# Decay gates of a gated linear attention: products in column and row groups, another copy on VectorE, and a new order of the first products

## The chip, the cores and the metric

The kernel runs on one core of a Trainium2 chip. The metric is the time of one execution on the device in microseconds (us). Three runs of the kernel before took 1970.91, 1971.70 and 1971.77; their median is 1971.7.

## The reference, cut to what matters

Two transformer blocks over 256 latent tokens of width 1024, all in float32. The first block reads 256 context tokens besides. Its mixer starts from one wide projection of the modulated, normalised tokens:

```python
h  = modulate(rms_norm(x_lat, norm1_g), sh1, sc1)      # latent tokens
hc = modulate(rms_norm(x_ctx, norm1_g), sh1c, sc1c)    # context tokens
q_c, kv_c, k_rope, gq, gk, gv, gr, glow, gate_logits = split_columns(h @ w_in)
# latent attention (MLA): q from rms_norm(q_c) @ w_uq, k and v from rms_norm(kv_c) @ w_ukv
lf, lb = glow[..., :16], glow[..., 16:]                # low-rank input of the decays, two directions
g_f = log_sigmoid(lf @ w_decay[0] + b_decay[0]) / 16   # 512 columns each
g_b = log_sigmoid(lb @ w_decay[1] + b_decay[1]) / 16
```

The decays g_f and g_b are summed over chunks and drive the gated linear attention (GLA). A feed-forward with a convolution follows. The second block has an attention, an mLSTM, a pooling mixer and two mixtures of 16 experts whose weights (2 x 16 x 12 MB) are all read.

## The kernel before, in words

Each engine runs one program written out by hand in its order; semaphores join them. Work waits for what stands ahead of it on its engine, so the order of the code is the order of time.

- **Banks.** `Groups` hands PSUM banks to products in turn: four in the first ring, four in a second one (`second=True`). `open` waits until the bank's last reader has given it back, `close` counts a product as done, `take` makes a reader wait for the product, `give` frees the bank, `read` waits until a bank has been given back.
- **Weights.** SyncE sends them in a fixed list into a ring of six slots of 2 MB. Each load waits until the product that last used its slot is done (`G.over`), or, where VectorE sums modulation columns itself (`mod_sum`), for that sum. The queue is in order.
- **First products.** TensorE transposes the tokens, forms four modulation rows (`mod`, L501) as their weights come, and sums squares (`norm`, L526). VectorE multiplies hT by gain and inverse root in tiles of 128 channels (L1787), latent tokens first; ScalarE adds the shift (L1389). Then come `kvr` (288 columns, four blocks of 128 tokens; blocks 0 and 1 are latent, 2 and 3 context), its root on ScalarE (L1423) and scaling on VectorE (L1837), transposes (`kvt`), `w_ukv` (eight products of two steps), `qc` (384 columns, latent blocks only), transposes of k and q, `w_uq`, rotary embedding. Ordinary chains of products all have line 475, transposes line 483.
- **Attention** over eight heads: scores (L555), softmax on VectorE and ScalarE, transposes (L483), outputs (L565), with products gk and gv as filling.
- **GLA.** After gv and gq, `low` is one product of 32 columns with all 512 tokens moving. VectorE copies it to SBUF (L1932) beside a row of ones, and the decays z (L696) are eight products of 33 rows: 16 of one direction, 16 of the other (zero weights stand where the other direction's are), and the bias. Each of the eight fills one bank; all eight banks are in use. For each half of four, ScalarE forms |z| (L1493), exp(-|z|) (L1495) and ln(1 + .) (L1496), and VectorE min(z,0) minus that, reading z from its bank (L1945) and giving it back. The product `gr` (L475, 64 instructions of 256 columns) takes the first four banks again. Then `tot` (L711) and the chunk sums.

A float32 product shows in the trace as two matmul instructions, so x64 are 32 products.

Of the kernel before, what the change touches and what calls it, by code (L numbers as in the profile page):

```python
# [8 lines left out]
ACT = mybir.ActivationFunctionType  # L9
ALU = mybir.AluOpType  # L10
# [3 lines left out]
D = 1024  # L14
KD = D // 128
# [238 lines left out]
def build(nc, w, consts, out):  # L254
# [3 lines left out]
    with ctx:  # L258
# [66 lines left out]
        sq_late = ar(0, KD, T)  # L325
        mrow = ar(17536, 512)

        kvr = ar(0, 4, 288)
# [17 lines left out]
        gex = ar(10240, 2, 512)  # L346
        wdec = ar(11264, 1024)
        qeT = ar(11264, 2, 4 * T)
        keT = ar(13312, 2, 4 * T)
        low = ar(15360, 512)  # L350
        dtm = ar(15872, 512)
        st = [ar(15360, 2, 512), ar(10240, 2, 512)]
        atT = ar(0, 8, 128)
        atM = ar(1024, 2, 256)
# [110 lines left out]
        def w3(v, k, n):  # L465
            return v[:, 0:k * n].rearrange("p (k n) -> p k n", k=k)
# [4 lines left out]
        def _(pe):  # L471
# [69 lines left out]
            def normed(c, k=KD):  # L541
                pe.wait_ge(sem("normed"), KD * (c - (c > 4)) + k)
# [60 lines left out]
            x = w3(weights(pe, "kvr"), KD, 288)  # L603
            for tb in range(4):
                if tb % 2 == 0:
                    normed(tb // 2)
                token_major("kvr", x, 288, tb)
            G.over("kvr")
            for j in range(2):
                b = G.open(pe, ("kvt", j))  # L610
                pe.wait_ge(sem("kv_norm"), 4)
                turn(("kvt", j), b, [kvr[:, tb, j * 128:j * 128 + 128] for tb in range(4)])
# [8 lines left out]
            G.over("w_ukv")  # L621
            x = w3(weights(pe, "qc"), KD, Q_LORA)
            for tb in range(TB):
                token_major("qc", x, Q_LORA, tb)
            G.over("qc")
            pe.wait_ge(sem("k_rope"), 4)
# [59 lines left out]
            b = G.open(pe, "low")  # L686
            chain("low", b[0:32, :], lambda k: x[:, k, :], lambda k: hT[:, k, :], KD)
            G.over("low")
            mod_columns(11)

            pe.wait_ge(sem("decay_in"), 3 * 16)
            pe.wait_ge(sem("low_ready"), 1)
            for tb in range(4):
                for d in range(2):
                    b = G.open(pe, ("z", tb, d), second=tb >= 2)
                    G.close(pe.matmul(b, low[0:33, tb * 128:tb * 128 + 128], wdec[0:33, d * 512:d * 512 + 512],  # L696
                                      start=True, stop=True), ("z", tb, d))
            x = w3(weights(pe, "gr"), KD, 512)
# [8 lines left out]
            for tb in range(TB):  # L707
                for d in range(2):
                    G.read(pe, ("z", tb, d))
                    r = 32 * (2 * tb + d)  # L710
                    ins = pe.matmul(b[r:r + 32, :], c_("chunk_pick"), gg[:, tb, d * 512:d * 512 + 512],  # L711
                                    start=True, stop=True, skip_group_check=True)
            G.close(ins, "tot")

            def context_sums(tb, d):
                b = G.open(pe, ("aft", tb, d))
                far = (tb, d) in ((2, 0), (3, 1))
                G.read(pe, ("z", tb, d))
                ins = pe.matmul(b, c_(("sum_after", "sum_before")[d]), gg[:, tb, d * 512:d * 512 + 512],
                                start=True, stop=not far)  # L720
                if far:
                    G.read(pe, ("z", 5 - tb, d))
                    ins = pe.matmul(b, c_("sum_all"), gg[:, 5 - tb, d * 512:d * 512 + 512], start=False, stop=True)
                G.close(ins, ("aft", tb, d))
# [627 lines left out]
        def _(act):  # L1352
# [23 lines left out]
            def root(c, then=None):  # L1376

                b = G.take(act, ("ms", c))
                if c:
                    act.wait_ge(sem("scaled"), KD * c)  # L1380
                G.give(act.activation(rs, b[:, 0:T], ACT.Sqrt, bias=eps, scale=1.0 / D), ("ms", c))
                if then:
                    act.activation(small[:, 4:5], one, then)
# [29 lines left out]
            squares(1, xcT)  # L1413
            for i in (1, 2, 3):
                mod(i)
            shift(0, mc(0, 0), hT[:, :, 0:T])
            root(1)
            shift(1, mc(0, 0, 1), hT[:, :, T:2 * T])
# [8 lines left out]
            for tb in range(4):  # L1427
                rms_root("kvr", tb, KV_LORA, KV_LORA, 8)
            for j in range(2):
                evict(("kvt", j), kvT[:, j, :], ACT.Copy, scale=vc("kv_norm_g", j))  # L1430
            for tb in range(4):
# [3 lines left out]
                G.give(act.copy(v_tm[:, tb, 256:512].rearrange("p (h c) -> p h c", h=4), v[:, :, NOPE:]), ("kv", tb, 1))  # L1435
            for tb in range(TB):
                rms_root("qc", tb, Q_LORA, Q_LORA, 12)
            for h in (1, 3):
# [41 lines left out]

            act.wait_ge(sem("wdec_cleared"), 1)
            act.dma_start(wdec[0:16, 0:512], w["gla_w_decay"][0, 0]).then_inc(sem("decay_in"), 16)
            act.dma_start(wdec[16:32, 512:1024], w["gla_w_decay"][0, 1]).then_inc(sem("decay_in"), 16)
            act.dma_start(wdec[32:33, :], w["gla_b_decay"].rearrange("a b c -> a (b c)")).then_inc(sem("decay_in"), 16)
            evict(("gv", 3), gv[:, 3, :])
            mod(12)
            evict(("gq", 1), gq[:, 1, :], scale=128 ** -0.5)
            mod(13)

            for half in range(2):  # L1490
                for tb in (2 * half, 2 * half + 1):
                    for d in range(2):
                        link(act.activation(gg[:, tb, d * 512:d * 512 + 512], G.take(act, ("z", tb, d)), ACT.Abs))  # L1493
                g = gg[:, 2 * half:2 * half + 2, :]
                link(act.activation(g, g, ACT.Exp, scale=-1.0))  # L1495
                act.activation(g, g, ACT.Ln, bias=one).then_inc(sem("gate_log"), 1)  # L1496
# [226 lines left out]
        def _(dve):  # L1723
# [54 lines left out]

            def invert(c):
                G.read(dve, ("ms", c))  # L1780
                link(dve.reciprocal(rs, rs))

            def norm(c, src, g, dst):
                if c:
                    invert(c)
                for k in range(KD):
                    dve.scalar_tensor_tensor(dst[:, k, :], src[:, k, :], g[:, k:k + 1], rs,  # L1787
                                             ALU.mult, ALU.mult).then_inc(sem("scaled"), 1)
# [33 lines left out]
            invert(0)  # L1822
            for i in (1, 2, 3):
                mod(i)
            set_gain(0, mc(0, 1), vc("norm1_g", 0, KD))
# [15 lines left out]
            for tb in range(4):  # L1841
# [6 lines left out]
                if tb < TB:  # L1848
                    link(rope(src.rearrange("p (n x h q) -> p n x h q", n=1, x=2, h=2),
                              src.rearrange("p (n x h q) -> p n x h q", n=1, x=2, h=2), "rope32", tb, small[:, 128:384], 1, 8))  # L1850
                dve.tensor_copy(kcat[:, tb, :].rearrange("p (h c) -> p h c", h=MLA_H)[:, :, NOPE:],
                                src.unsqueeze(1).to_broadcast([128, MLA_H, ROPE])).then_inc(sem("k_rope"), 1)
            for tb in range(4):
                b = G.take(dve, ("kv", tb, 0))
                v = b.rearrange("p (h c) -> p h c", h=4)
                dve.tensor_copy(kcat[:, tb, 0:4 * QH].rearrange("p (h c) -> p h c", h=4)[:, :, 0:NOPE], v[:, :, 0:NOPE])
                G.give(dve.tensor_copy(v_tm[:, tb, 0:256].rearrange("p (h c) -> p h c", h=4), v[:, :, NOPE:]), ("kv", tb, 0))
            for tb in range(TB):
                low_rank("qc", tb, qc[:, tb, :], Q_LORA, 12, "q_norm")
                dve.sem_inc(freed[G.bank[("qc", tb)]], 1)  # L1860
            for h in (0, 2):
# [58 lines left out]

            dve.memset(wdec[0:33, :], 0.0).then_inc(sem("wdec_cleared"), 1)
            mod_sum(10, 0, KD)
# [7 lines left out]
            b = G.take(dve, "low")  # L1930
            dve.memset(low[32:33, :], 1.0)
            G.give(dve.tensor_copy(low[0:32, :], b[0:32, :]), "low")  # L1932
            G.read(dve, "low")
            dve.sem_inc(sem("low_ready"), 1)
            mod_columns(11)
            for i in range(4, 12):
                G.read(dve, ("mod_t", i))

            def log_gates(half):

                dve.wait_ge(sem("gate_log"), half + 1)
                for tb in (2 * half, 2 * half + 1):
                    for d in range(2):
                        g = gg[:, tb, d * 512:d * 512 + 512]
                        G.give(dve.scalar_tensor_tensor(g, G.take(dve, ("z", tb, d)), 0.0, g, ALU.min, ALU.subtract),  # L1945
                               ("z", tb, d))

            log_gates(0)
            for j in range(3):
# [538 lines left out]
```

## Time and profile before

| | |
|---|---|
| runs, us | 1970.91, 1971.70, 1971.77 |
| profiled execution, us | 1969.03 |
| its span, us | 1967.2 |
| busy, us: TensorE, VectorE, ScalarE | 1654.7, 627.3, 406.9 |
| TensorE's mean granted clock | 0.903 |

The span runs from the first to the last instruction of the profiled execution; its own time is 1.8 us more. Busy time says how long an engine worked, not whether the end waited for it. The clock is given as a share of 2.4 GHz.

### The profile page before, as it was taken

Reading aid. Unit: us, or ns where it says so; the run is one execution under the profiler, and the core shown is the slowest. Engines: PE = TensorE matmul, PEld = TensorE weight load, DVE = VectorE, ACT = ScalarE, POOL = GpSimd, SP = SyncE. Lnnn points to the kernel's source line nnn. Section 1 sums busy time; section 2 is a strip of 40 time slices with the busy share of each in tenths; the row PEclk is TensorE's granted clock in tenths of the full one; section 3 lists DMA queues with packets and bytes.
Section 4 is the critical chain, followed back from the end, with each engine's and each line's share of the span. In section 5 each row is a group of like instructions: output and inputs, shape, how many; then the busy total and the mean of one; then the engine's idle time right before and its main releaser. Section 6 shows DMA issues by size and latency. Waiting matters only on the chain.

```text
span 1967.2 us, 22134 instructions
## 1 busy us (share of the span) xinstructions
PE 1654.7 (84%) x9130; PEld 1060.5 (54%) x9130; DVE 627.3 (32%) x1467; ACT 406.9 (21%) x717; POOL 18.6 (1%) x26
## 2 busy tenths in 40 slices
PE   6999999989999999996889676677687976776776
PEld 4544457878888886553645243243245533433433
DVE  3267344127798436546221000000024100000001
ACT  3221151011220023212132121121123211211211
POOL 0000000000110000000000000000000000000000
PEclk8999899999999999887879898898897988888888
DMA  9525740265639825105589999999996999999996
GB/s 366 179 98 202 282 162 1 86 221 186 218 125 359 320 101 206 43 1 215 224 336 430 428 429 428 429 429 428 428 366 256 397 429 428 429 428 429 428 428 262
DMA packets 110759, 572.47 MB, mean 291 GB/s; under 512 B 9153, under 2 KB 15425, under 8 KB 86114
## 3 DMA queue, kind: packets, MB, share of 16 engines
q1 hardware_dynamic: 109776, 569.79, 71.9%
q10 hardware_dynamic: 914, 1.72, 0.3%
q8 instruction: 49, 0.80, 0.2%
q14 instruction: 20, 0.16, 0.0%
HBM read 570.44 MB, written 1.05 MB: 291 GB/s over the span
## 4 chain that ended last, share of the span: by engine, by line
PE 61%; DMA 30%; DVE 4%; ACT 2%; issue 1%; SPq 1%; DVEq 0%; ACTq 0%
DMA ring<-in_w_exp_up_dram 29%; PE bank L475 20%; PE bank L1155 9%; PE bank L858 8%; PE bank L885 4%; PE bank L483 2%; PE bank L1181 2%; PE bank L1231 1%; PE bank L1191 1%; PE bank L901 1%; PE bank L555 1%; PE bank L501 1%; PE bank L526 1%; PE bank L1142 1%; DMA ring<-in_w_ada_dram 1%
## 5 line engine op out<-in xcount | busy, mean ns | idle before, releaser
L1155 PE MATMUL bank<-ring,arena 128*32 128x512 f32 x1792 | 264.1, 744 | 194.2 <-DMA ring<-in_w_exp_up_dram 192.2
L1155 PEld LDWEIGHTS bank<-ring,arena 128*32 128x32 f32 x1792 | 69.6, 133 | 386.1 <-issue 349.9
L2422 DVE COPY arena<-bank 128x256 f32<-128x256 f32 x32 | 13.6, 425 | 601.6 <-PE bank L1171 601.6
L475 PE MATMUL bank<-ring,hT 128*128 128x512 f32 (+4 forms) x480 | 163.6, 498 | 6.5 <-issue 4.9
L858 PE MATMUL bank<-hT,ring 128*128 128x256 f32 x704 | 156.5, 385 | 4.2 <-ACT hT L1389 4.2
L858 PEld LDWEIGHTS bank<-hT,ring 128*128 128x128 f32 x704 | 135.4, 193 | 23.3 <-issue 4.6
L475 PEld LDWEIGHTS bank<-ring,hT 128*128 128x128 f32 x480 | 88.1, 195 | 77.4 <-issue 67.3
L1181 PE MATMUL bank<-ring,arena 128*32 128x512 f32 x960 | 124.6, 664 | 1.7 <-DVE arena L2426 1.7
L1689 ACT COPY arena<-bank 128x512 f32<-128x512 f32 x32 | 33.4, 1045 | 435.9 <-PE bank L1155 435.9
L1191 PE MATMUL bank<-arena 128*128 128x256 f32 x512 | 118.8, 385 | 1.8 <-DVE arena L2434 1.8
L1761 DVE SCALAR_TENSOR_TENSOR spare<-ring,spare 128x512 f32<-128x512 f32 x154 | 116.3, 755 | 4.4
L1191 PEld LDWEIGHTS bank<-arena 128*128 128x128 f32 x512 | 94.6, 190 | 39.8 <-issue 28.2
L1142 PE MATMUL bank<-arena 128*128 128x32 f32 x960 | 110.2, 274 | 0.0
L1142 PEld LDWEIGHTS bank<-arena 128*128 128x128 f32 x960 | 110.1, 193 | 0.0
L475 PE MATMUL bank<-hT,ring 128*128 128x256 f32 (+1 forms) x464 | 109.8, 396 | 0.2 <-DVE arena L1945 0.2
L475 PE MATMUL bank<-arena,ring 128*128 128x256 f32 x416 | 97.2, 389 | 5.2 <-DVE arena L2012 3.5
L475 PEld LDWEIGHTS bank<-hT,ring 128*128 128x128 f32 (+1 forms) x464 | 88.8, 192 | 23.1 <-issue 10.9
L483 PE MATMUL bank<-cst,arena 128*128 128x128 f32 (+2 forms) x382 | 63.8, 311 | 41.9 <-DVE arena L1899 11.6
L2046 DVE SCALAR_TENSOR_TENSOR arena<-arena,vcol 128x256 f32<-128x256 f32 x176 | 91.9, 522 | 6.3
L475 PEld LDWEIGHTS bank<-arena,ring 128*128 128x128 f32 x416 | 81.2, 196 | 17.9 <-issue 4.8
L483 PEld LDWEIGHTS bank<-cst,arena 128*128 128x128 f32 (+2 forms) x382 | 49.8, 156 | 75.2 <-issue 64.2
L1365 ACT ACTIVATE arena<-bank 128x256 f32<-128x256 f32 (+2 forms) x72 | 32.3, 453 | 244.4 <-PE bank L475 136.4
(332 smaller groups left out, 1673.5 us busy)
## 6 DMA issues: line engine op xcount, KB each, us to landing
ring<-in_w_exp_down_dram SPq DMA_DIRECT2D x60, 2048.0 KB, 18.9
ring<-in_w_exp_gate_dram SPq DMA_DIRECT2D x56, 2048.0 KB, 19.0
ring<-in_w_exp_up_dram SPq DMA_DIRECT2D x56, 2048.0 KB, 23.4
ring<-in_w_mod_dram SPq DMA_DIRECT2D x24, 2048.0 KB, 12.4
ring<-in_w_ada_dram SPq DMA_DIRECT2D x12, 2048.0 KB, 13.2
ring<-in_w_up_dram SPq DMA_DIRECT2D x10, 2048.0 KB, 11.1
ring<-in_w_in_dram SPq DMA_DIRECT2D x8, 2048.0 KB, 13.6
arena<-in_w_exp_up_dram SPq DMA_DIRECT2D x6, 2048.0 KB, 22.6
```

Of the source, the lines that this page charges most:

```text
L475: ins = pe.matmul(b, lhs(k), rhs(k), start=(k == 0), stop=(k == n - 1))
L483: ins = pe.transpose(b[0:m, j * p:j * p + p], src, ident[0:p, 0:p])
L858: ins = pe.matmul(b[:, 0:T], x[:, k, j * 128:j * 128 + 128], hT[:, k, 0:T], start=(k == 0), stop=(k == KD - 1))
L885: ins = pe.matmul(acc[n // 2][:, (n % 2) * T:(n % 2) * T + T], x[:, k, n * 128:n * 128 + 128], ff[:, j, :], start=(j == 0 and n % 2 == 0), ...
L1142: ins = pe.matmul(bank[0][:, k * CAP:(k + 1) * CAP], h_tm[:, tb, k * 128:k * 128 + 128], hot[:, tb, :], start=(k + tb == 0), stop=(k == KD ...
L1155: ins = pe.matmul(bank[0][32 * q:32 * q + 32, :], xe[:, k * CAP:(k + 1) * CAP], xs[q // 2][:, o:o + 512], start=(k == 0), stop=(k == KD - ...
L1181: ins = pe.matmul(bank[2 + h][32 * q:32 * q + 32, :], act_t[:, 4 * j + q, :], x[:, q, h * 512:h * 512 + 512], start=(j == 0), stop=(j == 1 ...
L1191: ins = pe.matmul(acc[n // 2][:, (n % 2) * T:(n % 2) * T + T], dsb[:, n // 4, (n % 4) * 128:(n % 4) * 128 + 128], gates, start=False, stop ...
L1365: G.give(act.activation(to, src, func, **kw), name)
L1689: act.copy(gu.rearrange("p (k c) -> p c k", k=4), bank[0].rearrange("p (c k) -> p c k", k=4)).then_inc(sem("gu_copied"), 1)
L1761: ins = dve.scalar_tensor_tensor(a, x[:, k, :], cond[:, which, k, 0:1], a, ALU.mult, ALU.add)
L2046: ins = dve.scalar_tensor_tensor(y, win, tap(i, j), y, ALU.mult, ALU.add)
```

## The change

1. `kvr` is done tile by tile: both latent blocks of a channel tile as soon as that tile is ready, then both context blocks.
2. `qc` moves ahead of `kvt` and `w_ukv`, on TensorE, ScalarE and VectorE alike.
3. The root of the context norm gets a tile of its own (`rs_ctx`) and moves ahead of modulations 2 and 3, as does its reciprocal.
4. `low` is formed in four column groups: group 2 * par + d holds direction d for the token blocks of parity par. Four copies (two on VectorE, two on ScalarE) take it to SBUF, where a memset has put ones.
5. The decay weights and biases are loaded four times, once under each group, in eight loads instead of three. The products z have 17 rows at partitions 0, 32, 64, 96 in turn.
6. VectorE copies min(z,0) of each decay product to SBUF behind its |z| (`clip_gates`, for both halves ahead of `log_gates`) and gives the bank back there. `log_gates` then subtracts SBUF from SBUF. ScalarE no longer waits between one |z| and the next.

```diff
@@ TensorE, first products
-            for tb in range(4):
-                if tb % 2 == 0:
-                    normed(tb // 2)
-                token_major("kvr", x, 288, tb)
+            for half in range(2):
+                bs = [G.open(pe, ("kvr", 2 * half + t)) for t in range(2)]
+                for k in range(KD):
+                    normed(half, k + 1)
+                    for t in range(2):
+                        tb = 2 * half + t
+                        ins = pe.matmul(bs[t][:, 0:288], hT[:, k, tb * 128:tb * 128 + 128], x[:, k, 0:288],
+                                        start=(k == 0), stop=(k == KD - 1))
+                        if k == KD - 1:
+                            G.close(ins, ("kvr", tb))
             G.over("kvr")
+            x = w3(weights(pe, "qc"), KD, Q_LORA)
+            for tb in range(TB):
+                token_major("qc", x, Q_LORA, tb)
+            G.over("qc")
@@ TensorE, low and z
-            chain("low", b[0:32, :], lambda k: x[:, k, :], lambda k: hT[:, k, :], KD)
+            for k in range(KD):
+                for r in range(4):
+                    par, d = r // 2, r % 2
+                    tokens = hT[:, k, :].rearrange("p (a b t) -> p a b t", a=2, b=2)[:, :, par, :]
+                    ins = pe.matmul(b[32 * r:32 * r + 16, 0:T], x[:, k, 16 * d:16 * d + 16], tokens,
+                                    start=(k == 0), stop=(k == KD - 1), skip_group_check=True)
+            G.close(ins, "low")
...
-            pe.wait_ge(sem("decay_in"), 3 * 16)
+            pe.wait_ge(sem("decay_in"), 8 * 16)
             pe.wait_ge(sem("low_ready"), 1)
+            pe.wait_ge(sem("low_ready_too"), 2)
             for tb in range(4):
                 for d in range(2):
+                    r, at_ = 32 * (2 * (tb % 2) + d), tb // 2 * 128
                     b = G.open(pe, ("z", tb, d), second=tb >= 2)
-                    G.close(pe.matmul(b, low[0:33, tb * 128:tb * 128 + 128], wdec[0:33, d * 512:d * 512 + 512],
-                                      start=True, stop=True), ("z", tb, d))
+                    G.close(pe.matmul(b, low[r:r + 17, at_:at_ + 128], wdec[r:r + 17, :], start=True, stop=True), ("z", tb, d))
@@ ScalarE
             root(0)
             squares(1, xcT)
-            for i in (1, 2, 3):
-                mod(i)
+            mod(1)
+            root(1)
+            mod(2)
+            mod(3)
             shift(0, mc(0, 0), hT[:, :, 0:T])
-            root(1)
...
-            act.wait_ge(sem("wdec_cleared"), 1)
-            act.dma_start(wdec[0:16, 0:512], w["gla_w_decay"][0, 0]).then_inc(sem("decay_in"), 16)
-            act.dma_start(wdec[16:32, 512:1024], w["gla_w_decay"][0, 1]).then_inc(sem("decay_in"), 16)
-            act.dma_start(wdec[32:33, :], w["gla_b_decay"].rearrange("a b c -> a (b c)")).then_inc(sem("decay_in"), 16)
+            for r in range(4):
+                d = r % 2
+                act.dma_start(wdec[32 * r:32 * r + 16, :], w["gla_w_decay"][0, d]).then_inc(sem("decay_in"), 16)
+                act.dma_start(wdec[32 * r + 16:32 * r + 17, :], w["gla_b_decay"][0, d:d + 1]).then_inc(sem("decay_in"), 16)
...
+            b = G.take(act, "low")
+            act.wait_ge(sem("low_set"), 1)
+            for r in (2, 3):
+                act.copy(low[32 * r:32 * r + 16, :], b[32 * r:32 * r + 16, 0:T]).then_inc(sem("low_ready_too"), 1)
...
-                        link(act.activation(gg[:, tb, d * 512:d * 512 + 512], G.take(act, ("z", tb, d)), ACT.Abs))
+                        act.activation(gg[:, tb, d * 512:d * 512 + 512], G.take(act, ("z", tb, d)), ACT.Abs).then_inc(
+                            sem("gate_abs"), 1)
+                act.wait_ge(sem("gate_abs"), 4 * half + 4)
@@ VectorE
-            dve.memset(wdec[0:33, :], 0.0).then_inc(sem("wdec_cleared"), 1)
+            dve.memset(low, 1.0).then_inc(sem("low_set"), 1)
...
-            dve.memset(low[32:33, :], 1.0)
-            G.give(dve.tensor_copy(low[0:32, :], b[0:32, :]), "low")
-            G.read(dve, "low")
+            dve.wait_ge(sem("low_set"), 1)
+            dve.tensor_copy(low[0:16, :], b[0:16, 0:T])
+            link(dve.tensor_copy(low[32:48, :], b[32:48, 0:T]))
             dve.sem_inc(sem("low_ready"), 1)
+            dve.wait_ge(sem("low_ready_too"), 2)
+            dve.sem_inc(freed[G.bank["low"]], 1)
...
+            def clip_gates(half):
+
+                for n in range(4 * half, 4 * half + 4):
+                    tb, d = n // 2, n % 2
+                    dve.wait_ge(sem("gate_abs"), n + 1)
+                    G.give(dve.tensor_scalar(z_low[n], G.take(dve, ("z", tb, d)), 0.0, None, ALU.min), ("z", tb, d))
+
             def log_gates(half):
...
-                        G.give(dve.scalar_tensor_tensor(g, G.take(dve, ("z", tb, d)), 0.0, g, ALU.min, ALU.subtract),
-                               ("z", tb, d))
...
+                    dve.tensor_tensor(g, z_low[n], g, ALU.subtract).then_inc(sem("log_gates"), 1)
+            clip_gates(0)
+            clip_gates(1)
             log_gates(0)
```

## Rows read from the trace of the kernel before

**Rows 1.** The page, part 4: the chain that ended last, shares by engine

```profile
PE 61%; DMA 30%; DVE 4%; ACT 2%; issue 1%; SPq 1%; DVEq 0%; ACTq 0%
```

**Rows 2.** The chain of waits in order of time: start us, us, what

```profile
44.09 18.84 PE bank L475 x64
...
64.74 0.64 PE bank L483 x4
...
66.81 26.00 PE bank L475 x64
92.84 0.59 ACT small L1423 x2
...
97.49 7.99 PE bank L475 x24
...
117.48 6.87 PE bank L475 x16
...
1063.48 34.72 DMA ring<-in_w_exp_up_dram
```

**Rows 3.** Waits of the SyncE queue, 0 to 320 us: total us, times, longest

```profile
SPq L1273 <- PE bank L475: 134.4, 9, 29.1
```

**Rows 4.** Timeline, 0 to 112 us: start us, us, engine, line, operation [idle before]

```profile
17.70 3.76 SPq L1273 DMA_DIRECT2D ring<-in_w_in_dram  x1
...
33.95 3.23 PE L501 MATMUL bank<-ring,spare 128*32 128x512 f32 x16 [2.86 <-DMA ring<-in_w_ada_dram]
...
40.17 3.25 DVE L1787 SCALAR_TENSOR_TENSOR hT<-xT,gain,rs 128x256 f32<-128x256 f32 x8
40.69 3.30 ACT L1389 ACTIVATE hT<-hT,modc 128x256 f32<-128x256 f32 x8 [2.23 <-DVE hT L1787]
...
82.32 10.48 PE L475 MATMUL bank<-ring,hT 128*128 128x384 f32 x32
```

**Rows 5.** DMA issues of kvr's weights: KB, median us from issue to landing

```profile
ring<-in_w_in_dram SPq DMA_DIRECT2D x1, 1152.0 KB, 19.2
```

**Rows 6.** Stretches: us, busy by engine (instructions), granted clock, DMA share, GB/s

```profile
50.00:51.00 1.00, 1.00 (x5) 0.83 (x4) 0.00 (x0) 0.00 (x0) 0.00 (x0) 0.86 1.05 387
...
62.93:66.81 3.88, 1.06 (x8) 0.88 (x9) 1.13 (x4) 2.04 (x5) 0.00 (x0) 1.00 0.69 208
107.20:108.30 1.10, 0.04 (x2) 0.06 (x2) 1.10 (x4) 0.58 (x1) 0.00 (x0) 1.00 0.91 315
...
227.57:234.55 6.98, 6.98 (x17) 1.67 (x16) 0.16 (x1) 0.00 (x0) 0.00 (x0) 1.00 1.05 387
...
238.00:251.60 13.60, 13.40 (x21) 6.03 (x20) 2.48 (x4) 11.09 (x12) 0.00 (x0) 0.50 0.92 348
```

**Rows 7.** The chain of waits again, 225 to 305 us

```profile
227.64 6.98 PE bank L475 x16
...
248.44 15.65 PE bank L475 x64
...
270.44 0.99 PE bank L711 x8
...
301.61 1.09 PE bank L792 x16
```

**Rows 8.** Timeline, 234 to 262 us

```profile
235.29 0.68 DVE L1932 COPY arena<-bank 32x512 f32<-32x512 f32 x1
...
236.12 12.12 PE L696 MATMUL bank<-arena 33*128 33x512 f32 x16 [0.52 <-issue]
...
237.25 0.60 ACT L1493 ACTIVATE arena<-bank 128x512 f32<-128x512 f32 x1 [9.71 <-PE bank L696]
...
247.28 2.46 ACT L1493 ACTIVATE arena<-bank 128x512 f32<-128x512 f32 x4
247.60 2.48 DVE L1945 SCALAR_TENSOR_TENSOR arena<-bank,arena 128x512 f32<-128x512 f32 x4 [11.33 <-ACT arena L1496]
...
254.27 2.00 ACT L1496 ACTIVATE arena<-arena,small 128x2048 f32<-128x2048 f32 x1
```

More of the change, by code:

```diff
@@ L326, in build @@
         mrow = ar(17536, 512)
+        rs_ctx = ar(16512, T)
         kvr = ar(0, 4, 288)
@@ L346, in build @@
         gex = ar(10240, 2, 512)
-        wdec = ar(11264, 1024)
+        wdec = ar(11264, 512)
         qeT = ar(11264, 2, 4 * T)
         keT = ar(13312, 2, 4 * T)
-        low = ar(15360, 512)
+        low = ar(15360, T)
         dtm = ar(15872, 512)
         st = [ar(15360, 2, 512), ar(10240, 2, 512)]
+        z_low = [ar(11776 + 512 * i, 512) for i in range(7)] + [ar(10240, 512)]
         atT = ar(0, 8, 128)
@@ L621, in _ @@
             G.over("w_ukv")
[L622 to L625, printed above, removed]
             pe.wait_ge(sem("k_rope"), 4)
@@ L708, in _ @@
                 for d in range(2):
-                    G.read(pe, ("z", tb, d))
+                    pe.wait_ge(sem("log_gates"), 2 * tb + d + 1)
                     r = 32 * (2 * tb + d)
@@ L717, in context_sums @@
                 far = (tb, d) in ((2, 0), (3, 1))
-                G.read(pe, ("z", tb, d))
+                pe.wait_ge(sem("log_gates"), 2 * tb + d + 1)
                 ins = pe.matmul(b, c_(("sum_after", "sum_before")[d]), gg[:, tb, d * 512:d * 512 + 512],
@@ L721, in context_sums @@
                 if far:
-                    G.read(pe, ("z", 5 - tb, d))
+                    pe.wait_ge(sem("log_gates"), 2 * (5 - tb) + d + 1)
                     ins = pe.matmul(b, c_("sum_all"), gg[:, 5 - tb, d * 512:d * 512 + 512], start=False, stop=True)
@@ L1378, in root @@
                 b = G.take(act, ("ms", c))
-                if c:
+                if c > 1:
                     act.wait_ge(sem("scaled"), KD * c)
-                G.give(act.activation(rs, b[:, 0:T], ACT.Sqrt, bias=eps, scale=1.0 / D), ("ms", c))
+                G.give(act.activation(rs_ctx if c == 1 else rs, b[:, 0:T], ACT.Sqrt, bias=eps, scale=1.0 / D), ("ms", c))
                 if then:
@@ L1428, in _ @@
                 rms_root("kvr", tb, KV_LORA, KV_LORA, 8)
+            for tb in range(TB):
+                rms_root("qc", tb, Q_LORA, Q_LORA, 12)
             for j in range(2):
@@ L1435, in _ @@
                 G.give(act.copy(v_tm[:, tb, 256:512].rearrange("p (h c) -> p h c", h=4), v[:, :, NOPE:]), ("kv", tb, 1))
-            for tb in range(TB):
-                rms_root("qc", tb, Q_LORA, Q_LORA, 12)
             for h in (1, 3):
@@ L1779, in invert @@
             def invert(c):
+                r = rs_ctx if c == 1 else rs
                 G.read(dve, ("ms", c))
-                link(dve.reciprocal(rs, rs))
+                link(dve.reciprocal(r, r))
             def norm(c, src, g, dst):
-                if c:
+                if c > 1:
                     invert(c)
                 for k in range(KD):
-                    dve.scalar_tensor_tensor(dst[:, k, :], src[:, k, :], g[:, k:k + 1], rs,
+                    dve.scalar_tensor_tensor(dst[:, k, :], src[:, k, :], g[:, k:k + 1], rs_ctx if c == 1 else rs,
                                              ALU.mult, ALU.mult).then_inc(sem("scaled"), 1)
@@ L1822, in _ @@
             invert(0)
-            for i in (1, 2, 3):
-                mod(i)
+            mod(1)
+            invert(1)
+            mod(2)
+            mod(3)
             set_gain(0, mc(0, 1), vc("norm1_g", 0, KD))
@@ L1852, in _ @@
                                 src.unsqueeze(1).to_broadcast([128, MLA_H, ROPE])).then_inc(sem("k_rope"), 1)
+            for tb in range(TB):
+                low_rank("qc", tb, qc[:, tb, :], Q_LORA, 12, "q_norm")
+                dve.sem_inc(freed[G.bank[("qc", tb)]], 1)
             for tb in range(4):
@@ L1857, in _ @@
                 G.give(dve.tensor_copy(v_tm[:, tb, 0:256].rearrange("p (h c) -> p h c", h=4), v[:, :, NOPE:]), ("kv", tb, 0))
-            for tb in range(TB):
-                low_rank("qc", tb, qc[:, tb, :], Q_LORA, 12, "q_norm")
-                dve.sem_inc(freed[G.bank[("qc", tb)]], 1)
             for h in (0, 2):
@@ L1937, in _ @@
                 G.read(dve, ("mod_t", i))
+            def clip_gates(half):
[3 more added lines that the diff above has]
+                    G.give(dve.tensor_scalar(z_low[n], G.take(dve, ("z", tb, d)), 0.0, None, ALU.min), ("z", tb, d))
             def log_gates(half):
                 dve.wait_ge(sem("gate_log"), half + 1)
-                for tb in (2 * half, 2 * half + 1):
-                    for d in range(2):
-                        g = gg[:, tb, d * 512:d * 512 + 512]
-                        G.give(dve.scalar_tensor_tensor(g, G.take(dve, ("z", tb, d)), 0.0, g, ALU.min, ALU.subtract),
-                               ("z", tb, d))
+                for n in range(4 * half, 4 * half + 4):
+                    tb, d = n // 2, n % 2
+                    g = gg[:, tb, d * 512:d * 512 + 512]
+                    G.read(dve, ("z", tb, d))
+                    dve.tensor_tensor(g, z_low[n], g, ALU.subtract).then_inc(sem("log_gates"), 1)
+            clip_gates(0)
+            clip_gates(1)
             log_gates(0)
```

## The prediction

> **What bounds the kernel now.** I read the shares of the chain of waits first: TensorE holds 61% of it, DMA 30% [rows 1]. Then the chain in order of time. From 1063 us on it alternates with waits for expert weights [rows 2]; ahead of that, DMA stands in it only at the start, where the last modulation weights arrive at 33.95 us [rows 4]. Between the two the SyncE queue waits for TensorE [rows 3], so loads follow the products: time saved early moves everything behind it forward, the expert stream too. All edits lie between 33.95 and 270.44 us, so the question is how much earlier the product "tot" (L711) starts.
>
> **First products (kvr, w_ukv, qc).** The first product starts at 44.09 [rows 2], when all eight latent tiles are ready. VectorE scales from 40.17, ScalarE shifts eight tiles from 40.69 in 3.30, 0.41 each [rows 4]. With a wait per tile the first one is enough: 40.69 + 0.41 = 41.10, 2.99 us earlier. The weights were issued at 17.70 and landed 19.2 later, at 36.9 [rows 4, 5]: no new wait. One tile now feeds two blocks, four instructions. 64 take 18.84, in the mean 0.29, so at least 1.2 us per tile against 0.41 from ScalarE: the pacing costs nothing. The context root and reciprocal move ahead of modulations 2 and 3, into the wait for DMA that ends at 33.95; the context tiles are ready near 47.3, and TensorE asks for them near 52.
>
> The clock was at half level (1.2 GHz) from the start of this product to 50.3 (mean 0.86 in 50 to 51), then full [rows 6]. I take the slow stretch, 6.2 us, as equally long after the earlier start: gain 2.99. If it ends at the same moment, the extra 3 us are half wasted: 1.5. If there is none, 3.1 more: 6.1.
>
> Behind it TensorE waited from 44.09 + 18.84 = 62.93 to 64.74 for the last kv normalisation, then 2.07 for transposes and two evictions until 66.81 [rows 2]. Now qc (10.48 us [rows 4]) stands there and hides the normalisation: +1.81. But ScalarE takes qc's root first (0.59 for the squares [rows 2], with the root 0.9), where the evictions used to begin 0.66 behind the first transpose: 2.3 instead of 2.07, -0.24. Behind w_ukv the last kv eviction now stands open ahead of the kT transposes; in return qc's own root and scaling are gone there. I add 0.85 to the eviction's end, 1.7 for four heads' transposes (16 at 0.43/4), 0.65 for a kT eviction, 1.35 for three of qcT: 4.55, against 97.49 - 66.81 - 26.00 = 4.68 [rows 2]. Gain 0.1.
>
> w_ukv started at half clock: 66.81 to 82.32 is 15.51 [rows 2, 4], where 32 instructions at 0.429 (16 in 6.87 [rows 2]) make 13.74. Ahead of it TensorE had worked 1.06 of 3.88 us [rows 6]. The hole is now 2.3 us, right behind 10 us of dense work; a hole of 1.1 us between transposes left the clock at 1.00 [rows 6]. I take full clock, +1.77; bounds 1.77 and -1.7 (slow twice as long). Sum so far: 2.99 + 1.81 - 0.24 + 1.77 + 0.1 = 6.4.
>
> The stretch from 62.93 to 66.81 held eight transposes, and half clock followed. The Trainium skill, "TensorE: Matmul & The Clock Gate", Part 4: PE-mode transpose, says that transposes do not count as the engine being busy in the same way. By that rule the new hole is longer than it looks, and the slow start of w_ukv may stay; that is among the rivals, worked out from the rows above.
>
> SyncE's loads: the slot of w_ukv, free at 82.3 before, comes free at its new end near 86.5, and the load behind it (qc's slot, free since 70) queues there. Attention starts near 104.5, and VectorE wants these columns several products later. Hidden, with over 20 us to spare.
>
> **Attention** is not touched. The decay loads behind it grow from three issues to eight on ScalarE's queue, some 0.5 each, 4 us. ScalarE's next work is the eviction of a product of 16 instructions (6.87 [rows 2]) that starts at the same time: hidden; without that cover 2.5.
>
> **Low product.** 16 instructions of 512 columns took 6.98 [rows 7]. Now there are 64 of 256 columns in four column groups: one by one 64 x 0.2145 = 13.7, four at a time 3.4. Column groups do run together: L711, 128x32 tiles of 512 columns, does 8 in 0.99 [rows 7], where 0.429 each would make 3.4. But no row that I read has pairs closer than L792, 16 in 1.09, 68 ns each [rows 7]. I take 64 x 0.068 = 4.35, nearest to that row: gain 2.63. Bounds 3.4 (gain 3.6) and 0.99/8 = 124 ns, 7.9 (loss 0.9).
>
> The Trainium skill, "TensorE: Matmul & The Clock Gate", Part 1, gives about 62 ns per matmul where software decodes; by that page an estimate would be 4.0 us. The row's 68 ns decides here.
>
> The copies of low: before, 234.62 (227.64 + 6.98) to 236.12, a memset and a copy of 0.68 for 512 columns in it [rows 7, 8]. Now the memset is done long before, and VectorE makes two copies of 256 columns, ScalarE two beside them; at 0.4 each 1.1 in all, bounds 0.8 and 1.5. Gain 0.4.
>
> **Decay products and gates, the largest term.** Call the start of z Z, 236.12 before. "gr" started at 248.44, Z + 12.32 [rows 7], because it needed the bank of z(0,0), which VectorE began to release at 247.60, after Abs, Exp and Ln of the half [rows 8]. Now VectorE's copy of min(z,0) releases it: first Abs at 237.25, Z + 1.13, 0.60 long; the copy 0.7, like L1945, which also reads 512 columns of a bank (2.48 for four) [rows 8]; 0.2 of semaphores: Z + 2.6. z itself must be done by then. Sixteen instructions at 0.429 are 6.9 one by one, 1.7 in four row groups, 3.4 at half clock or with only two overlapping, which would cost 0.8. L792 shows two row groups overlapping: 68 ns for a 128-column instruction, for which 0.429/4 = 107 is the time by itself [rows 7]. I take 2.6: gain 9.7. Bounds: 0.2 (z takes 12.1 as before [rows 8]) and 9.7.
>
> Behind that, gr to tot took 270.44 - 248.44 = 22.0 [rows 7], kept. Half clock held from 238.0 to 251.6 [rows 6], so gr began with 3.2 us of it. I keep its 15.65. Bounds 13.8 (full clock) and 17.1 (slow as long as the first product was).
>
> What is late next: the gates. The second half, with four Abs in a row and two table loads, took from 247.28 to 256.27, 9.0 [rows 8]; the first can't take longer now. So its Ln ends by Z + 1.1 + 9.0 = Z + 10.1, the second by Z + 19.1. VectorE's copies of the second half wait for its Abs (until Z + 13.3), with log_gates(0) (2.5) and three gr evictions queued behind them: done by Z + 17.2. log_gates(1) ends by Z + 21.7, gr 3 and modulation 13 behind it. tot is due at Z + 2.6 + 22.0 = Z + 24.6: 3 us of slack. The eight extra copies on VectorE (8 x 0.62 = 5) hide under it; without it the second half's would cost 2.5. gr's four banks hold their products until VectorE comes; modulation 14 wants the first near Z + 18.3, free by Z + 16.3.
>
> Total: 6.4 + 2.6 + 0.4 + 9.7 = 19.1. The profiled execution took 1969.03 (span 1967.2): 1949.9. The median of the runs, 1971.7, lies 2.7 above it; by the median 1952.6.
>
> **Rivals.**
> Small losses together: the clock's dip at w_ukv stays (1.8), the low product gains nothing (2.6) and gr is slow for 6.2 us (1.4): 1958.4. For it: the rows show it at both levels, and I can't time its changes. The dip alone makes 1954.4; I give it 0.35 by itself.
> Row groups do not overlap: a tile of 17 rows is a form that no row has. z takes 12 us at half clock again, gr gains 0.2: 1952.6 + 9.5 = 1962.1. Against it: L792.
> Slower: tiles of 16 columns and of 17 rows run one after another, at half clock. The low product takes 64 x 0.429 = 27.5, 20.5 more than before; z as just said. -6.4 - 0.4 - 0.2 + 20.5 = +13.5: 1985.2. Where z does not overlap either, it decides from (6.98 + 7.0)/64, about 220 ns per pair, on. Against it: L711 at 124 ns for 512 columns, and the clock stayed at 1.00 through 6.98 us of 32-column tiles [rows 6, 7].
> No effect: something I missed between 60 and 270 binds, say VectorE's sums at the end of attention. Against it: the products of the chain stand back to back there. Within 3.9 of before.
>
> **How the numbers follow.** Forecast 0.6 (own range 1948 to 1956), small losses 0.25, row groups 0.08, no effect 0.03, slower 0.04. Low end: gr at full clock (1.9), the low product in 3.4 (0.9) and an earlier rise of the clock in the first product (1.7) give 1948.1. High end between the second and third case, 1961. About 0.2% (3.9 us) is what a measurement tells from no change: faster 0.93, same 0.03, slower 0.04.
>
> **What would show it.** The first product from 41.1 with qc right behind it; w_ukv 2.3 behind qc, in 13.7; low, 64 instructions in 4.3; gr within 3 us of z; tot about 19 earlier; the first wait for expert weights at about 1044 instead of 1063. It would be wrong if gr starts at the old distance, if low lasts over 7 us, or if tot waits for VectorE.

## The result, and the profile after

The changed kernel takes 1951.05 us (median of four runs, 1948.14 to 1954.61) against 1971.31 for the kernel before (four runs, 1966.35 to 1971.77). The ratio is 0.9903, 95% interval 0.9886 to 0.9919: 19 us faster, between 16 and 22. The forecast was 1952.6. The profiled execution took 1950.72, its span is 1948.7, 18.5 less than before.

Part 4 of the page of the profile has the same shares as before, 61% for TensorE and 30% for DMA. Here is the chain of waits in order of time (start us, us, what). L477, L485, L503, L528, L557 and L567 are the helper lines that were L475, L483, L501, L526, L555 and L565; L612 is kvr, L699 the low product, L517 columns of a modulation, L712 the decay products z, L1439 ScalarE's squares of qc, L726 tot.

```profile
11.63 20.62 DMA ring<-in_w_ada_dram
...
39.79 18.55 PE bank L612 x64
58.34 10.33 PE bank L477 x32
68.69 0.59 ACT small L1439 x2
...
70.90 13.99 PE bank L477 x32
...
89.59 7.99 PE bank L477 x24
...
219.56 3.58 PE bank L699 x64
223.14 0.98 PE bank L517 x8
...
224.26 2.28 PE bank L712 x16
226.57 0.70 DVE arena L1971
...
227.41 16.89 PE bank L477 x64
...
250.65 1.00 PE bank L726 x8
...
305.78 79.13 PE bank L477 x352
...
1044.98 34.67 DMA ring<-in_w_exp_up_dram
```

The stage is shorter in the same kind of chain [rows 1]. qc (x32, 10.33) stands directly behind kvr, w_ukv (13.99) 2.23 behind qc, and gr 3.15 behind z, where it had stood 12.32 behind [rows 2, 7]. The same points of both chains, in us:

| from, to | before | after | gain | forecast |
|---|---|---|---|---|
| 0, arrival of the last modulation weights | 33.91 | 32.25 | 1.66 | 0 |
| first product starts | 10.18 | 7.54 | 2.64 | 2.99 |
| w_uq starts | 53.40 | 49.80 | 3.60 | 3.44 |
| low starts | 130.15 | 129.97 | 0.18 | 0 |
| z starts | 8.48 | 4.70 | 3.78 | 3.03 |
| gr starts | 12.32 | 3.15 | 9.17 | 9.7 |
| tot starts | 22.00 | 23.24 | -1.24 | 0 |
| end of the span | 1696.76 | 1698.05 | -1.29 | 0 |
| sum | 1967.2 | 1948.7 | 18.5 | 19.1 |

The 1.66 is the DMA's own variation: nothing of the change lies ahead of it, and in the fourteen profiles of this study that arrival lies between 32.2 and 34.3, in no order that follows the kernels. The last loss is in one piece, x352, with 77.91 before and 79.13 here. The mean clock over that stretch was 0.98 before and 0.96 after; these are the lines (us, busy by engine, granted clock, DMA share, GB/s), first before, then after:

```profile
325.58:404.59 79.01, 77.89 (x352) 67.95 (x352) 10.20 (x24) 5.38 (x14) 0.00 (x0) 0.98 0.14 54
```

```profile
305.78:386.02 80.24, 79.12 (x353) 68.79 (x353) 10.20 (x24) 5.38 (x14) 0.00 (x0) 0.96 0.14 53
```

The clock falls earlier there: 1.2 us into the piece before, but already in the wait ahead of it in the changed kernel, so that 5.9 us of the piece are at half clock instead of 3.3.

```profile
324.00:326.00 2.00, 0.42 (x2) 0.43 (x3) 1.29 (x2) 0.00 (x0) 0.00 (x0) 1.00 0.00 0
```

```profile
304.00:306.00 2.00, 0.22 (x1) 0.25 (x2) 1.46 (x3) 0.00 (x0) 0.00 (x0) 0.71 0.00 0
```

This loss goes with the one at gr. In the seven profiles of this study where gr takes 16.6 to 17.0 us, x352 takes 78.98 to 79.20; in the other seven, where gr takes 14.05 to 15.9, it takes 77.91. Kernels with the old gates and with the new ones stand on both sides, so it follows the clock and not the form of the gates. Why the one follows the other 60 us later no run shows.

From there on both chains run in step: the first wait for expert weights comes 18.50 earlier [rows 2], the end 18.5. Where the time went at gr, the stretches show:

```profile
224.00:226.50 2.50, 2.36 (x18) 1.35 (x17) 0.21 (x2) 1.11 (x3) 0.00 (x0) 0.97 1.03 380
226.50:228.00 1.50, 0.62 (x3) 0.54 (x3) 1.43 (x3) 1.47 (x3) 0.00 (x0) 0.50 1.05 388
...
232.00:234.00 2.00, 2.00 (x9) 1.63 (x8) 0.78 (x2) 2.00 (x4) 0.00 (x0) 0.71 1.05 387
```

The clock falls to 1.2 GHz at 226.4, at the end of z, and rises near 233.2: gr has 5.8 us of half clock, where it had 3.2 [rows 6]. And in the timeline VectorE's copies (L1971, L1980 is log_gates; columns as in [rows 8]):

```profile
225.39 2.06 ACT L1513 ACTIVATE arena<-bank 128x512 f32<-128x512 f32 x4 [1.43 <-PE bank L712]
226.57 2.48 DVE L1971 TENSOR_SCALAR arena<-bank 128x512 f32<-128x512 f32 x4 [2.10 <-PE bank L712]
...
232.61 2.04 ACT L1513 ACTIVATE arena<-bank 128x512 f32<-128x512 f32 x4
233.22 2.48 DVE L1971 TENSOR_SCALAR arena<-bank 128x512 f32<-128x512 f32 x4 [4.17 <-ACT arena L1513]
```

### The profile page after: what moved, and what is told of

Its sections match the earlier page's. It is cut to its first block, busy times and chain, and to the rows that moved or that the text cites. A ratio compares the mean times of both kernels' runs of the same rounds, so it can differ in the third digit from the quotient of the medians.

```text
span 1948.7 us, 22252 instructions
## 1 busy us (share of the span) xinstructions
PE 1640.7 (84%) x9178; PEld 1058.1 (54%) x9178; DVE 630.9 (32%) x1475; ACT 406.6 (21%) x719; POOL 18.5 (1%) x26
## 4 chain that ended last, share of the span: by engine, by line
PE 61%; DMA 30%; DVE 4%; ACT 2%; issue 1%; SPq 1%; DVEq 0%; ACTq 0%
DMA ring<-in_w_exp_up_dram 29%; PE bank L477 19%; PE bank L1170 9%; PE bank L873 8%; PE bank L900 4%; PE bank L485 3%; PE bank L1196 2%; PE bank L1246 2%; PE bank L1206 1%; PE bank L916 1%; PE bank L557 1%; PE bank L503 1%; PE bank L528 1%; PE bank L1157 1%; DMA ring<-in_w_ada_dram 1%
## 5 line engine op out<-in xcount | busy, mean ns | idle before, releaser
L873 PE MATMUL bank<-hT,ring 128*128 128x256 f32 x704 | 156.5, 385 | 4.2 <-ACT hT L1404 4.2
L873 PEld LDWEIGHTS bank<-hT,ring 128*128 128x128 f32 x704 | 135.4, 193 | 23.4 <-issue 4.6
L477 PE MATMUL bank<-ring,hT 128*128 128x512 f32 (+3 forms) x416 | 144.5, 502 | 1.6 <-DVE arena L2274 1.5
L477 PEld LDWEIGHTS bank<-ring,hT 128*128 128x128 f32 x416 | 73.9, 191 | 67.6 <-issue 61.7
L477 PE MATMUL bank<-hT,ring 128*128 128x256 f32 x448 | 104.1, 392 | 0.9 <-DVE arena L1971 0.9
L477 PE MATMUL bank<-arena,ring 128*128 128x256 f32 x416 | 98.4, 393 | 5.2 <-DVE arena L2048 3.5
L477 PEld LDWEIGHTS bank<-hT,ring 128*128 128x128 f32 x448 | 88.0, 197 | 19.0 <-issue 6.4
L485 PE MATMUL bank<-cst,arena 128*128 128x128 f32 (+2 forms) x382 | 63.0, 309 | 39.1 <-DVE arena L1924 11.6
L477 PEld LDWEIGHTS bank<-arena,ring 128*128 128x128 f32 x416 | 82.0, 198 | 18.2 <-issue 4.8
L485 PEld LDWEIGHTS bank<-cst,arena 128*128 128x128 f32 (+2 forms) x382 | 49.6, 156 | 72.2 <-issue 63.6
## 6 DMA issues: line engine op xcount, KB each, us to landing
ring<-in_w_exp_gate_dram SPq DMA_DIRECT2D x56, 2048.0 KB, 19.1
ring<-in_w_mod_dram SPq DMA_DIRECT2D x24, 2048.0 KB, 12.3
```

Source lines behind the costliest of these rows:

```text
L477: ins = pe.matmul(b, lhs(k), rhs(k), start=(k == 0), stop=(k == n - 1))
L485: ins = pe.transpose(b[0:m, j * p:j * p + p], src, ident[0:p, 0:p])
L873: ins = pe.matmul(b[:, 0:T], x[:, k, j * 128:j * 128 + 128], hT[:, k, 0:T], start=(k == 0), stop=(k == KD - 1))
```

## The experiments

The theory is that each term of the sum has its own mechanism: the early start, qc as cover for the normalisation, column groups that run together, and a bank that comes free early behind row groups that run together. The main rivals are that the copy alone or the row groups alone make the large term, and that the stages are bound elsewhere.

**The first products alone.** Parts 1 to 3 of the change on the kernel before; low, z and gates as before.

> Parts 1 to 3 of the change alone (kvr tile by tile, qc ahead of kvt and w_ukv, the context root early). Theory: the stages add up, so this part is worth 6.4 us as forecast (6.2 in the profile of the changed kernel, after its modulation weights had landed 1.65 us earlier): about 1965 us against 1971.3, w_uq starting near 91, w_ukv in 14.0 at full clock. Rival: what is won here is lost at attention, where VectorE's sums or a load bind: within 1 us of before.

Measured 1961.01 (ten runs), ratio 0.9961 (0.9949 to 0.9974): 7.7 us, between 5 and 10. From the arrival of the weights to w_uq the chain takes 54.6 us, against 63.6 before. w_uq starts at 87.4, not 91: the arrival was 1.1 early, and the last modulation product (1.92 instead of 3.23) and kvr (17.27) caught a faster clock. The chain:

```profile
38.91 17.27 PE bank L611 x64
...
68.74 13.99 PE bank L476 x32
...
240.08 15.66 PE bank L476 x64
...
262.10 0.99 PE bank L718 x8
```

Not all of these 9.0 us arrive. From w_uq to low are 131.9 us, against 130.2 before: attention's first product of 16 instructions takes 8.10 instead of 6.87, at half clock when it starts. What the clock gave at kvr it took back there, and that is not particular to this kernel: of the ten profiles with qc ahead, six have kvr in 15.8 to 17.4 and this stretch in 131.8 to 131.9, the four others kvr in 18.6 to 18.8 and the stretch in 130.0 to 130.1. With that, arrival to low is 7.2 us shorter than before (6.4 in the changed kernel), and from low on both stages take what they took (42.80 to tot in either). VectorE's sums and the loads hold nothing; the theory holds.

**Low, z and gates alone.** Parts 4 to 6 on the kernel before.

> Parts 4 to 6 alone (low in column groups, z in row groups, min(z,0) copied). Theory: 3.4 + 0.4 + 9.2 less 1.2 for gr's longer time at half clock, about 11.8 us: 1959.5, gr about 3.1 behind the start of z. Rival: the two halves of the change help each other (the clock's state carries over): then this one and the first-products kernel together differ from the whole change by more than 3 us.

Measured 1952.55 (four runs), ratio 0.9914 (0.9884 to 0.9943): 17 us, between 11 and 23, more than expected in the middle and wide. The profile is sharper. From arrival (32.91) to tot (257.20) it takes 224.3, from 236.5 before, 12.2 less; the first products alone 229.3, 7.2 less. Together 19.4, and the whole change 218.4, 18.1 less. Each half also stays in its own stage: from low to tot this kernel takes 30.76 (42.80 before, 31.09 in the whole change), from arrival to low 193.5 (193.7 before). The halves add up within what the clock varies; of the rival nothing is seen at that size. By the times the two effects sum to 1.25% against the whole's 0.97%. The difference of 0.28% is less than the intervals together allow (about 0.36%, 7 us), so times alone could not tell 3 us.

```profile
226.44 3.58 PE bank L692 x64
...
233.88 16.97 PE bank L476 x64
```

**The change without the copy of min(z,0).**

```diff
-            clip_gates(0)
-            clip_gates(1)
             log_gates(0)
...
-                    dve.tensor_tensor(g, z_low[n], g, ALU.subtract).then_inc(sem("log_gates"), 1)
+                    G.give(dve.scalar_tensor_tensor(g, G.take(dve, ("z", tb, d)), 0.0, g, ALU.min, ALU.subtract), ("z", tb, d))
```

> The changed kernel without VectorE's copy of min(z,0): log_gates reads z from its bank and gives it back there, as before. Theory: the bank is what gr waits for. It comes free after Abs, Exp, table load and Ln: 1.13 + 2.1 + 1.91 + 1.28 + 2.0 + 1.1, so gr starts about 9.6 behind z instead of 3.15: 6.4 us slower than the changed kernel, near 1957.5. Rival: the row groups alone carry the gain: within 1 us of the changed kernel.

Measured 1958.71 (seven runs), ratio 0.9949 (0.9930 to 0.9968), where the whole change has 0.9903. gr starts 9.88 behind z, and the chain in between is the one named (expected 9.6):

```profile
225.61 1.15 PE bank L712 x7
226.76 2.06 ACT arena L1513 x4
228.84 1.91 ACT arena L1517
230.76 1.28 ACT L1518
232.06 2.01 ACT arena L1518
...
234.65 0.70 DVE arena L1972
...
235.49 16.98 PE bank L477 x64
```

So of the 9.17 us of this term the copy is worth 6.7, with row groups given.

**The copy alone.** The kernel before with clip_gates and the new log_gates; low and z as they were.

> The kernel before with the copy of min(z,0) alone (low with 32 columns, z with 33 rows as before). Theory: z itself, one by one and at half clock, takes 12.1 us, so the bank is free but TensorE is not: gr at 12.3 behind z as before, time within 1 us of 1971.3. Rival: the copy alone carries the gain: gr near 7 behind z, 5 us or more faster.

Measured 1968.60 (ten runs), ratio 0.9994 (0.9978 to 1.0010): no gain. The bank is free, but TensorE is still at z:

```profile
237.68 12.57 PE bank L697 x16
250.25 16.96 PE bank L476 x64
```

Copy and row groups are each half of a lock. The row groups alone give 2.4 us here (12.3 to 9.9), the copy alone nothing, together 9.2.

**The low product group by group.** The two loops exchanged.

```diff
-            for k in range(KD):
-                for r in range(4):
+            for r in range(4):
+                for k in range(KD):
```

> The changed kernel with the low product's two loops exchanged: the eight steps of one column group behind each other, then the next group. The same 64 instructions with the same data. Theory: the gain of this product comes from neighbours that lie in different column groups. In one group they run one by one, 64 x 0.2145 = 13.7 us (7.0 at least, if only weight loads bound them) instead of 3.58: 10 us slower than the changed kernel, 1961. Rival: the short tiles themselves make it fast (16 columns of weights, 256 moving): 3.6 to 4.4 us, no change.

Measured 1953.19 (four runs), ratio 0.9923 (0.9897 to 0.9949). The same 64 instructions take 11.38 us instead of 3.58, so column groups that alternate are what makes this product fast; the rival falls. It is less than the 13.7 expected for one by one. And the kernel is only 2 to 4 us slower by the times, not 10: from low to tot it takes 4.9 us more, since z and gr then run at full clock, and the stretch x352 takes 77.91 instead of 79.13:

```profile
217.93 11.38 PE bank L699 x64
...
233.49 14.05 PE bank L477 x64
...
253.89 1.00 PE bank L726 x8
```

I had not expected that. The same kernel once more:

> The changed kernel with the low product group by group, a second look. The first showed the low product in 11.4 us instead of 3.6 but gr in 14.05, all at full clock, instead of 16.9. Theory: the 7.8 us longer low product keeps the clock up, so gr runs in 14 again. Rival: that was chance; gr takes 15.7 to 17.

Measured 1955.64 (one run). The low product took 11.37, gr 14.05 again. Twice is not a proof, but seven other profiles with z in row groups directly behind a 3.58 us low product and ahead of gr (the whole change twice, the gates alone, without the copy, copies doubled, and twice the version with gr in the second ring) all have half clock in gr.

**Each copy made twice.**

```diff
                     dve.wait_ge(sem("gate_abs"), n + 1)
+                    link(dve.tensor_scalar(z_low[n], G.take(dve, ("z", tb, d)), 0.0, None, ALU.min))
```

> The changed kernel with each of VectorE's eight copies of min(z,0) made twice. Theory: VectorE has slack, so most of 8 x 0.7 = 5.6 us is hidden. The bank of the first product comes 0.7 later (gr +0.7), log_gates(1) at most 2.8 later against a slack of about 3 (it ended near 243.7, tot needed it at 250.65): 0.7 to 1.5 us slower. Rival: VectorE bounds the stage since the change: 4 to 5.6 us slower.

Measured 1950.95 (four runs), ratio 0.9908 (0.9883 to 0.9932): no difference from the change that the times could show. gr starts 3.87 behind z, 0.72 later, and tot 22.94 behind gr, 26.81 behind z instead of 26.39: 0.4 us by the profile, below the 0.7 to 1.5 expected. VectorE has the slack; the rival of 4 us or more falls.

**Tile by tile without moving qc.** Parts 1 and 3 on the kernel before.

> The kernel before with kvr tile by tile and the early context root alone, qc where it was. Theory: the start moves 2.8 us ahead and the rest keeps its waits (1.8 for the normalisation and w_ukv's start at half clock, 1.8): about 2.8 us faster than before, 1968.5, w_uq near 94.7. Rival: the shorter idle time changes the clock behind it as well, or the context tiles are late: 0 to 1.5, or over 4.

Measured 1969.13 (ten runs), ratio 0.9986 (0.9971 to 1.0001): 2.8 us by the middle, by its interval perhaps none. The start moves up as forecast: from the arrival to the first product are 7.8 us, to w_uq 61.7 (63.6 before). w_ukv and qc take 25.85, so w_ukv's slow start is there:

```profile
40.52 18.28 PE bank L611 x62
...
63.94 25.85 PE bank L476 x64
```

With qc behind w_ukv the two took 26.00, 27.28, 27.21 and 25.85 us in four profiles. With qc ahead they took 10.33 and 13.98 or 13.99, 24.32 in all, in ten of ten. The dip of the clock at w_ukv is not luck, and qc's place removes it. With qc behind, the hole ahead of w_ukv was 3.9 us or more, with qc ahead 2.2. What the front gained is lost again in this profile: w_uq takes 9.63 instead of 7.99, gr 17.03 and x352 79.20, all by half clock. gr's clock varies without the change too, 15.65 and 15.66 in two profiles with the old gates and 16.96 and 17.03 in two others.

**gr in the second ring.** The changed kernel with the second half of z behind gr's second product.

```diff
+            decays(0)
             x = w3(weights(pe, "gr"), KD, 512)
             for j in range(4):
+                if j == 2:
+                    decays(1)
-                b = G.open(pe, ("gr", j))
+                b = G.open(pe, ("gr", j), second=True)
```

> The changed kernel with gr in the second ring of banks and the second half of z (context tokens) in the first ring behind gr's second product. Theory: gr then waits for no z bank and follows the first half of z directly, at about 1.2 instead of 3.15 behind its start; the second half of z (1.1 us) moves behind and costs the same: 0.9 us faster by the wait that is gone, and up to 2.9 more if the clock no longer falls at gr's start. 1947 to 1950. Rival: the clock falls all the same, and the second half of the gates starts later and then holds tot: no faster than the changed kernel.

Measured 1950.11 (four runs), ratio 0.9897 (0.9870 to 0.9923). tot starts 24.74 behind z instead of 26.39. Again, with the changed kernel on the same chip:

> The changed kernel once more, beside the two versions below on the same chip, for their difference and for a second look at its clock. Theory: the first half of z's gates, gr and tot keep their distances (gr 3.15 behind z, tot 26.4 behind z with half clock at gr's start), w_ukv in 14.0 again. 1951. Rival: w_ukv's dip is a matter of luck and returns here (15.5 or more).

> gr in the second ring, second half of z behind gr's second product, once more. Its first profile had tot 24.7 behind z, against 26.4 in the changed kernel. Theory: 1.5 us faster than the changed kernel on the same chip. Rival: no difference.

The changed kernel took 1950.43 (six runs), ratio 0.9888 (0.9869 to 0.9906); this one 1945.85 (four runs), 0.9867 (0.9845 to 0.9889). tot is 24.75 behind z, against 26.43. So the profile gives 1.7 us twice, and in both profiles x352 takes 77.91, another 1.2 us; by the times the intervals overlap. w_ukv took 13.99 and 13.98: the rival of luck falls once more.

```profile
223.73 1.43 PE bank L713 x8
225.16 8.79 PE bank L477 x32
233.95 1.07 PE bank L713 x8
235.03 7.11 PE bank L477 x32
...
248.48 0.99 PE bank L731 x8
```

The wait is gone, but the clock falls all the same, for a shorter time: gr's first half takes 8.79, of which 3.4 us are at half clock, its second 7.11 at full clock.

**gr's first product between low and z.**

> As the kernel before this, and gr's first product also moves ahead of z, into the wait for low's copies; the second half of z stands behind gr's third product. Theory: from low's end TensorE then has 0.98 of columns, 13.8 of gr, 2.3 of z and 6.35 of modulations, no wait: tot at 23.4 to 24.5 behind low's end, where the changed kernel needs 27.5 and the one above 25.8. The gates start 3.4 later but have that slack. 3 to 4 us faster than the changed kernel, near 1947.5; the dense product between the thin ones also leaves the clock at full level. Rival: the later gates hold tot (ScalarE copies modulation 14 only behind the second Ln): within 1 us of the changed kernel or slower.

Measured 1947.14 (five runs), ratio 0.9875 (0.9857 to 0.9894). That is 3.3 us less than the changed kernel on the same chip (1950.43). The clock stayed at full level: gr's first three products took 3.56 + 7.10 and the rest ran at the same pace; x352 took 77.91. But tot starts 25.43 behind low's end, not 23.4 to 24.5 (27.55 in the changed kernel beside it, 25.82 in the version above). The rival named the reason, though not the size; the chain goes through the gates:

```profile
226.54 3.56 PE bank L477 x16
230.10 1.07 PE bank L710 x8
231.18 7.10 PE bank L477 x32
...
239.39 2.04 ACT arena L1519 x4
...
245.97 2.01 ACT arena L1524
248.01 2.50 DVE arena L1986 x4
...
250.99 1.06 PE bank L732 x8
```

The second half of z, behind gr's third product, came 0.85 too late for ScalarE, and log_gates, the last gr eviction and modulation 13 hold the bank of tot. By the times it lies between its neighbours, the changed kernel and the version above, and can't be told from either.

## Why the prediction was right, point by point

**First product from its first tile.** Right, 2.65 instead of 2.99. The row of eight shifts gave 0.41 per tile, but that is their pipelined distance; the first alone takes 0.52, and the product starts 0.14 after it.

**qc as cover for the normalisation.** Right: no wait behind kvr. The hole behind qc, 2.23, was forecast at 2.3, and from w_ukv's end to w_uq are 4.70 (forecast 4.55).

**w_ukv at full clock.** Right: 13.98 or 13.99 in ten of ten profiles, where 13.74 was forecast. A hole of 2.2 us with eight transpose instructions in it, behind 10 us of dense work, never lowered the clock here. The rule on transposes of the Trainium skill, "TensorE: Matmul & The Clock Gate", Part 4: PE-mode transpose, that they don't count as busy in the same way, could have left the dip in place. It did not come, but that does not speak against the rule: counted as idle, the hole is still shorter than the 3.9 us that did lower the clock.

**Low product.** Forecast 4.35, measured 3.58, 56 ns per pair. I took the spacing of L792, 68 ns, as the nearest row for the issue rate; it is not the limit here. The trace has its weight loads, of 128 columns, at 188 ns each and those of low, of 16 columns, at 97; that the loads set the pace at L792 was not tested. The lower bound, 3.4, was the better value. The estimate of 4.0 from about 62 ns per matmul where software decodes (the Trainium skill, "TensorE: Matmul & The Clock Gate", Part 1) was too long as well; whether its condition holds here no run shows.

**Copies of low.** 223.14 to 224.26, 1.12: as forecast.

**The bank of z(0,0).** The mechanism is right and shown from both sides. 3.15 instead of 2.6: VectorE's first copy starts 1.18 behind the first Abs, where the second half's starts 0.61 behind. It was 0.83 in the two kernels that have the copy but the old first products. The cause is open. VectorE has a row of semaphore waits ahead of that copy, but they don't make the delay: with gr's first product ahead of z VectorE had over 4 us for them before the first Abs, and its copy still came 1.18 behind. z took 2.28, within what was allowed for it.

```profile
231.19 2.06 ACT L1519 ACTIVATE arena<-bank 128x512 f32<-128x512 f32 x4 [4.81 <-PE bank L710]
232.37 2.48 DVE L1977 TENSOR_SCALAR arena<-bank 128x512 f32<-128x512 f32 x4 [5.49 <-ACT arena L1519]
```

**gr to tot unchanged.** The step that was mis-sized: 23.24 instead of 22.0, all of it half clock in gr (16.89 instead of 15.65), inside the stated bounds (13.8 to 17.1).

**Slack of VectorE and ScalarE.** Right: log_gates of the second half ended at 243.7 (forecast Z + 21.7 at the latest, 246.0), tot at 250.65, and doubled copies cost nothing behind gr. The version with gr's first product ahead of z shows where that slack ends.

**Everything behind moves along.** Right to 0.1 us from 386 to the end of the span, expert stream included. At attention too: its chain does pass through VectorE's sums near the end, where the argument against "no effect" had the products back to back, but they start 92.85 us behind w_uq in both kernels. What the sum had at nothing is the clock at 306 (-1.22), the second part of what gr's slow start costs. An earlier arrival (+1.66) covers it in this pair of profiles, and that is luck: from the arrival to the end of the span the gain is 16.8, against 19.1 forecast. The second profile of the changed kernel has 18.0.

## What to carry to other kernels

Ask what holds a buffer, not only what computes: a short copy that lets a bank go early is worth its whole chain of readers, but only if the writer of that bank is out of the way too. Test such pairs each alone. Let small-tile products alternate between column or row groups from one instruction to the next; the same instructions group by group took three times as long. A dense product that is ready served twice here when it covered a wait: it hid the wait, and the clock stayed up for what followed. And where the clock falls behind a product that was made faster, look for the cost further on as well: here it came once at gr and once more at 306.

## What the runs showed of the hardware that I had not expected

- 64 float32 instructions of 16-column tiles with 256 moving columns, alternating over four column groups, took 3.58 us, 56 ns each. In one group after the other they took 11.38, 178 ns each, which is still less than the 220 ns that gr's 256-column instructions in full tiles take at full clock (14.05 us for 64).
- z in four row groups: 16 instructions of 512 columns in 2.28 us, 142 ns each, against the 429 that 512 columns take one by one in full tiles at full clock (6.87 us for 16).
- The clock fell right behind short low and z products (3.6 and 2.3 us with thin joins between them), and stayed up when the same low product was slowed to 11.4 us or a dense product stood between. A faster product gave some of its gain back to the next one: low gained 7.8 us against its slow form, gr lost 2.8 and the stretch x352 1.2.
